# A two-layer decoder trunk on one core: the preloaded expert pair and the shared product move in the expert loop, and small work changes places and engines around it

## The reference, cut to what matters

```python
def mix_even(x, ...):                     # layer 0
    z = x @ w_in                          # q, k, v, r, glr, u
    log_a = log_sigmoid(glr @ w_gk2 + b_gk) / 16
    o, s_gla_new = chunked_linear_attention(q, k, v, log_a, s_gla, 16)
    ...
def moe(x, ...):
    scores = sigmoid(x @ w_router)        # 64 experts, 8 per token, group-limited
    for e in experts:
        acc += gate[e] * ((silu(x @ wg[e]) * (x @ wu[e])) @ wd[e])
    return acc + (silu(x @ w_sg) * (x @ w_su)) @ w_sd
def trunk(x, ...):
    for i in range(2):
        x = layer_norm(ALPHA * x + mix(x));  x = layer_norm(ALPHA * x + moe(x))
        x = x + sigmoid(x @ w_ple_gate[i]) * (p[i] @ w_ple_proj[i])
```

## Time and profile before

| | |
|---|---|
| median of 3 runs | 1608.55 us (1607.81 to 1611.89) |
| the profiled execution | 1611.03 us |
| its span, first to last instruction | 1609.2 us |
| PE busy | 1562.5 us, 97% |
| DVE, ACT, POOL busy | 537.7, 339.4, 149.0 us |
| read from HBM | 526.15 MB, 342 GB/s over the span |
| matmuls of the expert loops, L1373 and L1402 | 408.9 and 226.5 us busy |

### The profile page before, as it was taken

How to read it: one execution, slowest core, us unless ns; L and a number is a source line. 1 busy time by engine, 2 the same in 40 slices (tenths; PEclk the granted TensorE clock), 3 DMA queues, 4 the chain that set the end, 5 groups by cost and what they waited for, 6 DMA issues and landing times.

```text
span 1609.2 us, 22408 instructions
## 1 busy us (share of the span) xinstructions
PE 1562.5 (97%) x8258; PEld 793.3 (49%) x8258; DVE 537.7 (33%) x1328; ACT 339.4 (21%) x688; POOL 149.0 (9%) x241
## 2 busy tenths in 40 slices
PE   7999899999999999999999999989999999999998
PEld 5775544344444443466665754554443444444435
DVE  2157522222222222351434335462222122222226
ACT  2211122121221221221222221022211122122222
POOL 0241100000000000000111011020000000000000
PEclk9999999999999999999999999999999999999999
DMA  9733999999989999973577586589999998999990
GB/s 293 271 115 152 361 402 420 420 421 419 419 362 420 420 420 419 386 264 105 177 241 242 192 281 236 200 344 403 421 420 420 414 417 352 421 420 420 421 366 30
DMA packets 121756, 536.18 MB, mean 333 GB/s; under 512 B 17897, under 2 KB 29545, under 8 KB 73936
## 3 DMA queue, kind: packets, MB, share of 16 engines
q1 hardware_dynamic: 98599, 470.88, 73.6%
q0 software_dynamic: 21216, 61.12, 10.5%
q10 hardware_dynamic: 1872, 3.22, 0.6%
HBM read 526.15 MB, written 23.87 MB: 342 GB/s over the span
## 4 chain that ended last, share of the span: by engine, by line
PE 84%; DMA 8%; DVE 5%; issue 1%; ACT 1%; SPq 1%; DVEq 0%; POOLq 0%; ACTq 0%
PE ps L1373 24%; PE ps L1402 12%; PE ps L1157 11%; PE ps L1187 9%; DMA weights<-in_w_exp_up 7%; PE ps L1313 6%; PE ps L1366 4%; PE ps L1309 2%; PE ps L1386 2%; PE ps L1395 1%; PE ps L1066 1%; DVE x_tok L2491 1%; PE ps L1563 1%; PE ps L1330 1%; PE ps L1044 1%
## 5 line engine op out<-in xcount | busy, mean ns | idle before, releaser
L1373 PE MATMUL ps<-weights,x_feat 128*64 128x512 f32 x1856 | 408.9, 593 | 10.9 <-DMA weights<-in_w_exp_up 8.4
L1373 PEld LDWEIGHTS ps<-weights,x_feat 128*64 128x64 f32 x1856 | 134.6, 137 | 276.0 <-issue 276.0
L1402 PE MATMUL ps<-weights,arena 128*64 128x512 f32 x992 | 226.5, 599 | 0.9 <-ACT arena L1593 0.9
L1157 PE MATMUL ps<-x_feat,weights 128*128 128x288 f32 x800 | 203.6, 412 | 1.1 <-ACT x_feat L1593 1.1
L1157 PEld LDWEIGHTS ps<-x_feat,weights 128*128 128x128 f32 x800 | 154.3, 195 | 43.6 <-issue 3.8
L2247 DVE CAST split<-state 128x1024 fp32r<-128x1024 f32 (+1 forms) x66 | 44.7, 677 | 325.0 <-ACT state L1593 325.0
L2244 DVE SCALAR_TENSOR_TENSOR arena<-arena,ps 128x256 f32<-128x256 f32 x64 | 30.8, 481 | 348.7 <-ACT arena L1823 348.7
L2644 POOL DMA_INDIRECT arena<-x_rows,arena x64 | 63.6, 994 | 876.7 <-DVE arena L2237 833.4
L1593 ACT ACTIVATE state<-ps 128x512 f32<-128x512 f32 x132 | 78.8, 597 | 283.6 <-PE ps L1402 261.2
L1402 PEld LDWEIGHTS ps<-weights,arena 128*64 128x64 f32 x992 | 65.7, 136 | 132.2 <-issue 130.9
L1823 ACT ACTIVATE arena<-ps 128x256 f32<-128x256 f32 x64 | 24.5, 383 | 430.7 <-PE ps L1373 404.3
(11 more groups left out here) (311 smaller groups left out, 1323.9 us busy)
## 6 DMA issues: line engine op xcount, KB each, us to landing
weights<-in_w_exp_gate SPq DMA_DIRECT2D x124, 1024.0 KB, 13.5
weights<-in_w_exp_up SPq DMA_DIRECT2D x124, 1024.0 KB, 16.5
weights<-in_w_exp_down SPq DMA_DIRECT2D x124, 1024.0 KB, 15.0
weights<-in_w_in_c SPq DMA_DIRECT2D x24, 1024.0 KB, 7.7
arena<-in_state_ret POOLq DMA_DIRECT2D x20, 512.0 KB, 5.2
out_ret_sample<-arena POOLq DMA_DIRECT2D x20, 512.0 KB, 6.4
weights<-in_w_in_a SPq DMA_DIRECT2D x8, 1024.0 KB, 10.2
weights<-in_w_ple_gate SPq DMA_DIRECT2D x8, 1024.0 KB, 18.1
```

Source lines behind the costliest of these rows:

```text
L1157: last = pe.matmul(ps[:, 0:T], lhs(c), XT[:, c, :], start=(c == 0), stop=(c == n - 1))
L1373: last = pe.matmul(ps[64 * s:64 * s + 64, :], XGT[u][:, c, 64 * s:64 * s + 64], rhs, start=(c == 0), stop=(c == KC - 1))
L1402: last = pe.matmul(ps[64 * s:64 * s + 64, :], HT[u][:, c, 64 * s:64 * s + 64], wd[s][:, c, 512 * n:512 * n + 512], start=(c == 0), stop=(c ...
```

## The change

Six edits:

- `HOME` is 10 instead of 16: the home pair is the eleventh of the loop.
- `shared_down` stands behind the 18th pair (`SHARED_AT = 9` double turns) instead of the 12th. The loops' bodies are split accordingly.
- `wglr` is 32 columns wide for each of the eight features groups, the upper 16 set to zero by GpSimd; L854 writes all 128 partitions and ScalarE copies them in one instruction.
- The keys of the sample chunk are masked by ScalarE in eight copies with a column scale, instead of by VectorE in one product.
- VectorE and ScalarE raise the phase before the affine of the sample columns, not behind it. Row affines: chunk 0 (layer 0) goes between the two halves of chunk 1's residual; the sample rows' product stands ahead of the last columns' affine, their sum behind it, and then chunk 1.
- GpSimd stores the chunks in the order 0, 2, 1.

```diff
-HOME = 16
+HOME = 10
+SHARED_AT = 9
...
-        gate_ops = a.take(8 * RANK + 256 + T)
+        gate_ops = a.take(8 * TS + 256 + T)
...
             for c in range(KC):
                 q = c % 4
-                last = pe.matmul(ps[TS * q:TS * q + RANK, 0:T], wglr[:, c, :], XT[:, c, :], start=(c < 4), stop=(c >= KC - 4))
+                last = pe.matmul(ps[TS * q:TS * q + TS, 0:T], wglr[:, c, :], XT[:, c, :], start=(c < 4), stop=(c >= KC - 4))
...
                 two_pairs(0)
-                with pe.Fori(1, HOME // 2 - 2) as it:
+                with pe.Fori(1, HOME // 2 - 1) as it:
                     two_pairs(it)
+                for it in range(HOME // 2 - 1, HOME // 2 + 1):
+                    two_pairs(it)
+                with pe.Fori(HOME // 2 + 1, SHARED_AT) as it:
+                    two_pairs(it, True)
                 shared_down()
-                for it in range(HOME // 2 - 2, HOME // 2 + 1):
-                    two_pairs(it)
-                with pe.Fori(HOME // 2 + 1, PROJECT_AT) as it:
+                with pe.Fori(SHARED_AT, PROJECT_AT) as it:
                     two_pairs(it, True)
                 early_projection()
...
                     full(act, ("glr",))
-                    act.wait_ge(sem("ones_set"), 1)
-                    for q in range(4):
-                        ins = copy(glrT[TS * q:TS * q + RANK, :], bank(("glr",))[TS * q:TS * q + RANK, 0:T])
-                        if q < 3:
-                            st.run(ins)
-                        else:
-                            st.free(ins, ("glr",))
+                    st.free(copy(glrT, bank(("glr",))[:, 0:T]), ("glr",))
...
+                    full(act, ("dS", 1, 1, 1))
+                    full(act, ("kdT", 2))
+                    act.wait_ge(sem("even_table"), 16)
+                    for i in range(8):
+                        ins = copy(KDM[0:TS, i, :], bank(("kdT", 2))[0:TS, 0:256], scale=mch_s[0:TS, i:i + 1])
+                        if i < 7:
+                            st.run(ins)
+                        else:
+                            st.free(ins, ("kdT", 2))
...
+                st.phase()
                 x_affine(f"xTb{l}", l, 1, ORD1[l][1:2])
-                st.phase()
...
-                mask_keys(j + 1)
+                if j == 0:
+                    mask_keys(1)
...
             x_affine(f"xTb{l}", l, 1, ORD1[l][2:])
-            dve.wait_ge(sem("ln_in", l, 1), 32)
-            for j in range(l % 2, 3):
-                affine(l, 1, j)
+            shift(l, 1, 2)
+            affine(l, 1, 1)
...
+            def stretch(l, k, j):
...
+                st.run(TT(x, x, norm_place(l, k)[0][0:r, :], ALU.mult))
...
+            def shift(l, k, j):
...
+                st.tell(TT(x, x, norm_place(l, k)[1][0:r, :], ALU.add), sem("x_affine", l, k))
...
+                            if j == 1 and n == 0:
+                                dve.wait_ge(sem("ln_in", l, 1), 32)
+                                affine(l, 1, 0)
...
+                st.phase()
                 x_affine(f"xTb{l}", l, 1, ORD1[l][1:2])
-                st.phase()
-                experts_dve(dve, st, TT, TSc, STT, l, x_affine, affine, norm, half_stats)
+                stretch(l, 1, 2)
+                experts_dve(dve, st, TT, TSc, STT, l, x_affine, affine, shift, norm, half_stats)
...
-            for j, (o, r) in enumerate(CH):
-                pool.wait_ge(sem("x_affine", l, 1), j + 1)
+            for i, j in enumerate(ORD):
+                o, r = CH[j]
+                pool.wait_ge(sem("x_affine", l, 1), i + 1)
                 store(xd[o:o + r, :], X[0:r, j, :], sem("x_rows"))
...
-            st.run(pool.memset(gate_ops[:, 128:384 + T], 0.0))
+            st.run(pool.memset(wglr[:, :, RANK:TS], 0.0))
+            st.run(pool.memset(wgk2, 0.0))
```

More of the change, by code:

```diff
@@ L357, in trunk @@
         SMb = sb("small", 556)
-        ASZ = 16830
+        ASZ = 16958
         TOP = ASZ - 2 * PW
@@ L405, in trunk @@
         own_strip = ce.take(1)
-        gate_ops = a.take(8 * RANK + 256 + T)
-        wglr = gate_ops[:, 0:128].rearrange("p (c n) -> p c n", c=8)
-        wgk2 = gate_ops[:, 128:384]
-        glrT = gate_ops[:, 384:384 + T]
+        gate_ops = a.take(8 * TS + 256 + T)
+        wglr = gate_ops[:, 0:256].rearrange("p (c n) -> p c n", c=8)
+        wgk2 = gate_ops[:, 256:512]
+        glrT = gate_ops[:, 512:512 + T]
         PUO = gate_ops[:, 0:512]
@@ L850, in even_pe @@
             pe.wait_ge(sem("gate_in"), 16 * 6)
+            pe.wait_ge(sem("ones_set"), 1)
             ps = begin(("glr",))
@@ L2157, in odd_dve, with experts_dve @@
                     affine(1, 1, 0)
-        def experts_dve(dve, st, TT, TSc, STT, l, x_affine, affine, norm, half_stats):
+        def experts_dve(dve, st, TT, TSc, STT, l, x_affine, affine, shift, norm, half_stats):
             R3 = [P, 3, E]
             x_affine(f"xTb{l}", l, 1, ORD1[l][2:])
-            dve.wait_ge(sem("ln_in", l, 1), 32)
-            for j in range(l % 2, 3):
-                affine(l, 1, j)
+            shift(l, 1, 2)
+            affine(l, 1, 1)
             dve.wait_ge(sem("tables_set"), l + 1)
@@ L2484, in norm @@
                 st.tell(TSc(x, x, bnag[0:r, 2 * j:2 * j + 1], rstd[0:r, j:j + 1], ALU.subtract, ALU.mult), done)
-            def affine(l, k, j):
+            def stretch(l, k, j):
                 r = CH[j][1]
@@ L2491, in affine @@
                 st.run(TT(x, x, norm_place(l, k)[0][0:r, :], ALU.mult))
+            def affine(l, k, j):
+                stretch(l, k, j)
+                shift(l, k, j)
+            def shift(l, k, j):
+                r = CH[j][1]
+                x = X[0:r, j, :]
                 st.after
```

3 lines of the change are left out of this document (1 added, 2 removed).

## The result

The changed kernel takes 1600.87 us (median of 6 runs, 1597.73 to 1602.20), the kernel before beside it 1610.81 us (6 runs, 1607.81 to 1614.02). The ratio is 0.9936, 95% interval 0.9922 to 0.9950: 10.3 us less, between 8.1 and 12.6. The forecast was 1592.0 us and the range ended at 1600. The way was right, the size was not: 16.5 us were summed up. The profiled execution has a span of 1598.6 us, 10.6 less than that of before.

What follows compares the result with a forecast made beforehand. TensorE, busy 97% of the span, was taken as the bound, its loops racing the weight stream. 1.3 + 6.0 + 3.0 + 0.8 + 5.4 = 16.5 us off 1611.03, less 2.5 for the median: 1592.0 us, range 1586 to 1600.

Steps and rivals of the forecast that it cites:

- Part 1: Start: one ScalarE copy of the gate's low-rank product instead of four lets TensorE start L860 1.3 us earlier.
- Part 2: Sample keys masked on ScalarE: TensorE's wait falls from 2.98 to 0.4 us and the clock stays up, 6.0 us.
- without the gap that work runs at 2.4 GHz: Behind the key products: work at 0.50 clock takes 3.35 us instead of 6.7 once the wait is gone.
- Part 3: Routing: sample columns behind the phase and affines in idle places save 3.0 us in layer 0, 0.8 in layer 1.
- Part 4: Expert loops: home pair eleventh, shared product behind the 18th pair save the waits of pairs 11 and 12, 5.4 us.
- the fourteenth again has about 7.9: Loops: behind the new home pair, the weights' lead at the fourteenth pair is back at about 7.9 us.
- From there both are alike, with the same waits at the end: Loops: from the 25th pair, with a lead of 1.3 us in both kernels, the waits at the end are equal.
- rival 3: Waits only move to the loops' end; at 16.05 us per pair the 5.4 us are gone: 1597.4 us, chance 0.17.
- The level: The whole kernel before: its profiled execution, 1611.03 us, lies 2.5 us above the median of three runs, 1608.55.
- Rival 1: More clock at layer 1's phase (3.35 us) and the start's matmuls (1.7 us): 5.1 us more, 1586.9 us, chance 0.13.
- rival 4: Slower: interval per pair in the loops at 16.5 us, 21.6 us lost against 16.5 gained, 1613.6 us, chance 0.03.
- rival 2: Key products: the gap stays over 0.8 us and the clock falls, 4 us less gained, 1596.0 us, chance 0.12.

Runs made afterwards that it cites:

- Experiment 3: The changed kernel with the sample keys masked by VectorE again: 1608.24 us, ratio 0.9982.
- Experiment 12: The changed kernel with phase, row affines and stores ordered as in the kernel before: 1602.17 us, ratio 0.9952.
- experiment 9: The changed kernel with the projection's second transfer cut in two: 1 and 127 rows, 1649.87 us; 16 and 112 rows, 1608.54 us.
- experiment 2: The changed kernel with the loops and home pair place of the kernel before: 1600.45 us, ratio 0.9934.
- experiment 6: The kernel before with the change's loops alone and 60 idle instructions on TensorE's sequencer: 1608.79 us, ratio 0.9982.
- experiment 1: The kernel before with the change's loops alone: 1610.42 us, ratio 0.9997.
- experiment 11: The changed kernel with 60 idle TensorE instructions and all gate and up panels cut by the contraction: 1612.60 us, ratio 1.0007.
- 13: The changed kernel with the low-rank product copied in four instructions of 32 partitions each: 1603.11 us, ratio 0.9952.

## Why the prediction was wrong, point by point

**Part 1** was right: 1.79 to 0.52 us, 1.3 us earlier.

**Part 2** was right in its mechanism. The copies took 370 ns each, less than the row of 470 ns that bounded them, and the wait is 0.02 us, not 0.4. The step "without the gap that work runs at 2.4 GHz" was half right: in the profiled execution 3.4 us at 0.50 remain, so the two traces show 4.6 us: from the score matmuls at 92.10 to 117.65 before, from 90.25 to 111.23 after, where the next dense product starts:

```profile
117.65 1.88 PE L1227 MATMUL ps<-weights,arena 128*128 128x512 f32 x4
```

```profile
111.23 2.31 PE L1228 MATMUL ps<-weights,arena 128*128 128x512 f32 x5
```

Experiment 3 measures 7.4 us by timing, known to some 3, and the forecast of 6.0 lies between. The rule of the Trainium skill ("ScalarE: Activation LUTs", section "Rules for kernel authors") that multiplications belong on VectorE would have left this wait as it was. Here the engine that was idle at the right time won, at a longer busy time (2.96 us against 2.27).

**Part 3** was right in size by the two traces: 9.57 - 6.42 (the next dense products, 117.65 to 111.23) = 3.15 us in layer 0 against 3.0, with the row gather as the new wait, as forecast (1.44 us). In this the trace of after was lucky: that the 0.50 stretch behind the count product goes holds in it, but in nine of the twelve kernels with this routing a longer wait for the gather is followed by a stretch of the same length, and most of 1.7 us is lost again. Experiment 12, by timing, has 2.6 us for both layers, known to some 3. In layer 1 the first gathered rows come 9.68 us earlier after 9.28 at 966.23 and 956.95: 0.4 us against 0.8.

**Part 4** was wrong in layer 0, and it is the step that broke the forecast: "the fourteenth again has about 7.9" and "From there both are alike, with the same waits at the end". The lead is the time from a panel's last landing to the start of its pair. In layer 0 the fourteenth pair, which starts at 363.25 us with a panel landed at 356.91, had 6.3 us. At the 25th the changed kernel had 536.34 - (511.14 + 21.0) = 4.2 us, the kernel before 549.08 - (523.88 + 19.2) = 6.0 (both above the forecast's 1.3, which left out the projection's matmuls ahead of this pair). First after, then before:

```profile
536.34 7.09 PE L1374 MATMUL ps<-weights,x_feat 128*64 128x512 f32 x32
...
weights<-in_w_exp_up SPq DMA_DIRECT2D x1, 1024.0 KB, 21.0
```

```profile
549.08 7.09 PE L1373 MATMUL ps<-weights,x_feat 128*64 128x512 f32 x32
...
weights<-in_w_exp_up SPq DMA_DIRECT2D x1, 1024.0 KB, 19.2
```

These 1.8 us less are the 1.8 us by which the waits at the loop's end grew. So the two saved waits are indeed gone, and rival 3 is what happened in layer 0: from the landing at 356.91 us to that at 645.00, 18 pairs on, the interval was 16.0 us, not 15.9, by the rival's own price 1.8 us a loop.

Where the stream's gain went is seen in the 32 raises of the loop's last gate and up panel (experiment 9 explains them). Times are counted in layer 0 from the loop's first product, in layer 1 from its first down product:

| | layer 0 before | after | layer 1 before | after |
|---|---|---|---|---|
| mean of the 32 raises, us | 465.7 | 462.1 | 457.2 | 453.1 |
| last raise, us | 470.7 | 470.0 | 462.4 | 459.3 |
| last behind the mean, us | 5.0 | 7.9 | 5.2 | 6.2 |

On the mean the weights came 3.6 and 4.1 us earlier, in layer 0 as much as the queue's pauses say. But the last part, for which TensorE waits, came only 0.7 and 3.1 us earlier, which is what the two loops gained. The rest, 2.9 and 1.0 us, lies in parts that landed early for nothing. What the rival named as its reason, a queue that never pauses, fits: the raises spread wider from pair to pair, and draw together where the queue pauses. Behind the old home pair, where 5.3 us of the stream are lost, the spread falls from 9.1 to 4.3 us; behind the new one in layer 0, where only 1.5 are lost, from 7.9 to 5.8. What makes one part of a transfer slower than another is open.

In layer 1 the step held: at the 25th pair the leads are 5.9 and 5.8 us, and the loop saved 3.1 us against 2.7. Part of that may be the execution: experiment 2, with the loops of before, needs 474.4 us for this stretch, not 476.3.

The sum left out a second thing altogether: **that moved code can have to be waited for**. The new loops made TensorE's program longer, and a jump behind layer 1's loop now costs 1.9 us. Measured: loops 2.9 us without that wait (experiment 6), 0.5 with it (experiment 1), 5.4 forecast.

**The level** was taken wrong by 2.2 us: the profiled execution of before was put 2.5 us above the median of three runs, but the median over all runs beside these experiments is 1610.1 to 1611.2 us. Three runs were too few to correct a profile by. Of the 8.9 us between 1592.0 and 1600.87 the level is 2.2; the rest is gain that did not come.

**Layer 1's start** lost 1.0 us: 6.7 us at 0.50 instead of 3.3 around the same waits, of 0.9 and 1.1 us. Experiment 2 shows none there, nor do 11 and 13, and the rest 3.4 or 6.8 us around the same waits, so this is the execution, not the change.

So of the two traces' shortfall, 16.5 - 10.6 = 5.9 us, 3.5 are the loops and the code behind them (1.9 for 5.4), 1.4 the clock behind the keys, 1.0 that at layer 1's start; the smaller differences cancel. The 1.4 and the 1.0 belong to these two executions, the 3.5 is borne out by experiments 1, 2 and 6. Rival 1 (more clock) and rival 4 (an interval of 16.5 us) did not come; of rival 2 only the clock, without the wait it was meant to follow from.

## What to carry to other kernels

A lead that is saved in the middle of a loop is worth something only if it is still there at the loop's end: follow the bytes to the last part of the last landing, and count where the stream stands still, not where the engine waits. Before reading a landing off a profile, see whether two transfers raise one semaphore: then their landings are not told apart. When a program's loops are cut differently, look at the first instruction behind each loop for a wait that no data ends, and try a shift of the code before giving up on the edit. A small product that stands behind a long queue on its engine can gain much on a slower engine that is idle, here 7.4 us by timing (4.6 by the traces) for 2.3 us of work, because the clock fell with the wait.

## What was not expected of the hardware

- A transfer of 1 MB raises its semaphore in sixteen steps, and in a stream that never runs dry these steps drift apart: the 32 raises of a 2 MB panel spread over 3.0 us early in layer 0's loop (issued at 195.51) and over 13.0 us at its end; a pause of the queue draws them together. What makes it is open, and so is what the loops would gain without it, since no run took it away.
- A transfer of 1 row and one of 127 rows of 4 KB made TensorE wait 18.4 and 19.7 us; 16 and 112 rows did not. In the traces the transfers of 128, 16 and 112 rows raise their semaphore sixteen times each, those of 1 and 127 rows twice each, once within 0.5 us of the issue; the last of these raises came 44 us after the issue of the 127 rows.
- Panels of the same size, cut into rows of 4 KB instead of 8 KB, moved 412 instead of 420 GB/s, and the kernel, whose loops are bound by the stream, took 13 us longer (experiment 11).
- The jump past code that is rarely run cost 1.5 to 2.0 us or nothing with only the place of the program changed, and 3.54 or 4.45 us in another place of the two shorter programs; TensorE went on 2.4 to 2.7 us after an instruction transfer began.
